# The MLP's first matrix on rows not yet multiplied by the norm's root, with the shift as two more moving columns

## The reference, cut to what matters

```python
x = x + gate1 * (merged @ w_o[l])

u2 = rmsnorm(x, norm_mlp[l]) * (1.0 + scale2) + shift2
h = jnp.square(jax.nn.relu(u2 @ w_ff1[l]))
x = x + gate2 * (h @ w_ff2[l])
```

## Time and profile before

| | us |
|---|---|
| three runs | 982.01, 984.34, 984.48 |
| median | 984.34 |
| span of the profiled execution (first to last instruction) | 980.8 |
| PE busy | 934.8 (95%) |
| POOL busy | 739.2 (75%) |
| DVE busy | 665.4 (68%) |
| ACT busy | 492.7 (50%) |

### The profile page before, as it was taken

One profiled execution on the slowest core, in us unless ns is written; L12 is line 12 of the kernel. 1 busy time (PEld: TensorE's weight loads), 2 busy tenths in 40 slices (PEclk: granted clock), 3 DMA queues, 4 the chain that ended last, 5 costly groups with the idle time before them and its releaser, 6 DMA issues.

```text
span 980.8 us, 21945 instructions
## 1 busy us (share of the span) xinstructions
PE 934.8 (95%) x7758; PEld 909.3 (93%) x7758; DVE 665.4 (68%) x1097; ACT 492.7 (50%) x811; POOL 739.2 (75%) x894
## 2 busy tenths in 40 slices
PE   6999899999789999999999999999989999999996
PEld 6898789999779999999899999999988999999996
DVE  4979996765877774652566678886466666888722
ACT  3455556654346665554454455444454444544441
POOL 1486565677687999998677659999956676799973
PEclk9999999999999999999999999999999999999999
DMA  9985555646453557565354444555515444455521
GB/s 374 401 321 178 212 177 210 236 152 246 164 192 130 204 190 273 179 216 209 129 172 155 150 166 172 174 192 194 211 45 178 167 171 155 146 192 194 178 101 43
DMA packets 28222, 185.20 MB, mean 189 GB/s; under 512 B 3027, under 2 KB 5504, under 8 KB 6272
## 3 DMA queue, kind: packets, MB, share of 16 engines
q1 hardware_dynamic: 25832, 167.93, 47.5%
q10 hardware_dynamic: 2328, 16.40, 4.6%
HBM read 183.26 MB, written 1.07 MB: 188 GB/s over the span
## 4 chain that ended last, share of the span: by engine, by line
PE 74%; DVE 16%; issue 5%; ACT 3%; DMA 1%; DVEq 1%; POOL 0%; SPq 0%; POOLq 0%; ACTq 0%
PE mm L544 21%; PE mm L545 21%; PE mm L546 21%; ACT w_hi L1001 1%; PE mm L578 1%; DVE cy L1967 1%; DVE w_lo L1406 1%; PE mm L562 1%; DVE cy L1972 1%; PE ps_s L871 1%; DVE qr L1991 1%; PE ps_o L888 1%; PE ps_o L962 1%; DVE rt L1990 1%; DVE mix_lo L1936 1%
## 5 line engine op out<-in xcount | busy, mean ns | idle before, releaser
L470 POOL TENSOR_TENSOR w_lo<-raw,w_hi 128x256 fp32r<-128x256 f32 x876 | 729.7, 869 | 215.4 <-ACT w_hi L1001 212.9
L544 PE MATMUL mm<-u_hi,w_hi 128*128 128x256 f32 x1616 | 462.2, 286 | 4.6 <-issue 4.4
L545 PE MATMUL mm<-u_lo,w_hi 128*128 128x256 f32 x1616 | 449.5, 278 | 0.0
L546 PE MATMUL mm<-u_hi,w_lo 128*128 128x256 f32 x1616 | 449.4, 278 | 0.0
L1001 ACT ACTIVATE w_hi<-raw 128x1024 fp32r<-128x1024 f32 x291 | 306.2, 1058 | 144.1 <-PE mm L546 139.6
L544 PEld LDWEIGHTS mm<-u_hi,w_hi 128*128 128x128 f32 x1616 | 304.9, 189 | 12.4 <-issue 11.9
L545 PEld LDWEIGHTS mm<-u_lo,w_hi 128*128 128x128 f32 x1616 | 304.0, 188 | 2.0 <-issue 1.9
L546 PEld LDWEIGHTS mm<-u_hi,w_lo 128*128 128x128 f32 x1616 | 304.4, 188 | 0.0
L1406 DVE TENSOR_TENSOR w_lo<-raw,w_hi 128x1024 fp32r<-128x1024 f32 x72 | 103.4, 1436 | 58.0 <-ACT w_hi L1001 55.4
L544 PE MATMUL mm<-mix_hi,w_hi 128*128 128x256 f32 x256 | 71.7, 280 | 1.5 <-DVE mix_lo L1976 1.5
L545 PE MATMUL mm<-mix_lo,w_hi 128*128 128x256 f32 x256 | 71.4, 279 | 0.0
(11 more groups left out here) (292 smaller groups left out, 1331.1 us busy)
## 6 DMA issues: line engine op xcount, KB each, us to landing
raw<-weights SPq DMA_DIRECT2D x145, 1024.0 KB, 4.8
ada_raw<-ada ACTq DMA_DIRECT2D x14, 1024.0 KB, 5.3
ada_raw<-ada SPq DMA_DIRECT2D x6, 1024.0 KB, 12.4
ada_more<-ada SPq DMA_DIRECT2D x4, 1024.0 KB, 12.7
bias<-tab_scratch SPq DMA_DIRECT2D x1, 1536.0 KB, 9.3
dec<-decay ACTq DMA_DIRECT2D x1, 1536.0 KB, 8.8
x<-xT SPq DMA_DIRECT2D x1, 1024.0 KB, 9.9
out<-x SPq DMA_DIRECT2D x4, 256.0 KB, 2.3
```

Of the source, the lines that this page charges most:

```text
L470: ins = nc.gpsimd.tensor_tensor(w_lo[:, s, at], r[:, at], hi[:, at], ALU.subtract)
L544: nc.tensor.matmul(dst, wh, rhs_hi(k), start=a, stop=False)
L545: nc.tensor.matmul(dst, wh, rhs_lo(k), start=False, stop=False)
L546: i = nc.tensor.matmul(dst, wl, rhs_hi(k), start=False, stop=b)
```

## The change

With a = gain * (1 + scale2), u2 @ w is r * ((a x) @ w) + shift2 @ w. So:

- `u_hi`/`u_lo` now hold a x, without r and without shift. ACT (from x, scale `a_mix`) and DVE (`row_lo`, L1509) write them slice by slice within the w_o product. `make_u` and `make_u_hi` are gone.
- Two more columns stand behind the 256 tokens in each slice of u: shift2 (hi and lo) and zero. Each of the 768 matmuls of the first matrix moves 258 columns; the 257th output column is shift2 @ w.
- PE goes from the w_o product straight into the first two units. The statistic's matmuls stand behind the seventh slice of these, the spread behind the third unit. No `keep_warm` there.
- In `up_turn` DVE copies the 257th column to `wsum`, and multiplies the bank by r (kept in `row1`) into `z_h`, which lies in PSUM; ACT takes relu(z + wsum) from there, squares it, and only then makes the next `w_hi`. DVE makes `h_full` = (z + wsum) * relu, in PSUM too, and `h_lo`.
- The eight sums of gate2's row move into turns 2, 4, 6, 8, 14, 16, 20, 22 of the first matrix, their two loads behind turns 7 and 10 of ACT. DVE's loop over the turns is written out in full, ACT's by half.

```diff
+U_PITCH = T + 32
+U_WIDE = T + 2
...
-    u_hi = keep("u_hi", [P, KC, T], F32R)
-    u_lo = keep("u_lo", [P, KC, T], F32R)
+    u_hi_all = keep("u_hi", [P, KC, U_PITCH], F32R)
+    u_lo_all = keep("u_lo", [P, KC, U_PITCH], F32R)
+    u_hi, u_lo = u_hi_all[:, :, 0:T], u_lo_all[:, :, 0:T]
...
-    h_full = p2("h_full", [P, 2, T])
+    row1 = p2("row1", [P, T])
+    wsum = p2("wsum", [P, 2, 1])
...
+    z_h = ps_s[0].rearrange("p (e t) -> p e t", e=2)
+    h_full = ps_t[:, :].rearrange("p (e t) -> p e t", e=2)
...
+    GATE2_AT = [2, 4, 6, 8, 14, 16, 20, 22]
+    GATE2_LOAD = {7: 22, 10: 23}
...
-                    dst = mm[oo % 4][:, 0:T]
+                    dst = mm[oo % 4][:, 0:w]
...
-        norm_stat(1, O_F1)
-
-        first_units(2, U_F1, O_F1, u_ready(1))
-
+        def stat_behind(k):
+
+            if k == KC - 2:
+                stat(1)
+
+        uhw = lambda k: u_hi_all[:, k, 0:U_WIDE]
+        ulw = lambda k: u_lo_all[:, k, 0:U_WIDE]
+        pe.wait_ge(S["shift_zero"], 2)
+        pe.wait_ge(S["shift_lo"], 1)
+        first_units(2, U_F1, O_F1, u_ready(1), behind=stat_behind, w=U_WIDE)
         for i in range(2, 8):
-            unit(None, U_F1 + i, O_F1 + i, uh, ul)
+            unit(None, U_F1 + i, O_F1 + i, uhw, ulw, w=U_WIDE)
+            if i == 2:
+                spread(1)
         with pe.Fori(0, 3) as g:
             for i in range(8):
-                unit(g, U_F1 + 8 + i, O_F1 + 8 + i, uh, ul)
+                unit(g, U_F1 + 8 + i, O_F1 + 8 + i, uhw, ulw, w=U_WIDE)
...
-            high(None, U_WO + j + SLOTS)
-            if j in (2, 4):
-                ada_load(act, 21 + j // 2)
+            if j == 0:
+                ada_read(act, 5 * KC - 1)
+                A(u_hi_all[:, :, T], mod[:, SHIFT2, :], ACT.Copy).then_inc(S["shift_hi"], 1)
+            if j < KC - 1:
+                high(None, U_WO + j + SLOTS)
             act.wait_ge(taken[o % 4], o // 4 + 1)
+            A(u_hi[:, j, :], x[:, j, :], ACT.Identity, scale=a_mix[:, 1, j:j + 1]).then_inc(S["uhi_ready"], 1)
             square_x(1, j, x[:, j, :])
+        high(None, U_F1 + SLOTS - 1)
         root(1)
-        ada_read(act, 4 * KC - 1)
-        make_u_hi(1, SHIFT2)
 
 
         def up_turn(g, base):
             for i in range(8):
                 c, o, f = U_F1 + base + i, O_F1 + base + i, base + i
-                act.wait_ge(S["unit_done"], lin(g, 8, c + 1))
                 if f >= 2:
                     act.wait_ge(S["hl_ready"], lin(g, 8, f - 1))
-                A(relu_h[:, f % 2, :], mm[o % 4][:, 0:T], ACT.Relu).then_inc(taken[o % 4], 1)
-                high(g, c + SLOTS)
+                act.wait_ge(S["wsum_ready"], lin(g, 8, f + 1))
                 act.wait_ge(taken[o % 4], lin(g, 2, o // 4 + 1))
+                A(relu_h[:, f % 2, :], z_h[:, f % 2, :], ACT.Relu, bias=wsum[:, f % 2, 0:1]).then_inc(S["relu_made"], 1)
+                act.wait_ge(S["relu_made"], lin(g, 8, f + 1))
                 dst = h_hi[:, f, :] if g is None else h_hi[:, bass.ds(g * 8 + f, 1), :][:, 0, :]
                 A(dst, relu_h[:, f % 2, :], ACT.Square).then_inc(S["hh_ready"], 1)
-
-        up_turn(None, 0)
-        with act.Fori(0, 3) as g:
-            up_turn(g, 8)
+                high(g, c + SLOTS)
+                if g is None and f in GATE2_LOAD:
+                    ada_load(act, GATE2_LOAD[f])
...
+        for tile in (u_hi_all, u_lo_all):
+            V.memset(tile[:, :, T + 1].bitcast(F32), 0.0).then_inc(S["shift_zero"], 1)
...
+            if j == 1:
+                dve.wait_ge(S["shift_hi"], 1)
+                V.tensor_tensor(u_lo_all[:, :, T], mod[:, SHIFT2, :], u_hi_all[:, :, T].bitcast(F32), ALU.subtract)\
+                    .then_inc(S["shift_lo"], 1)
+            if j:
+                row_lo(1, j - 1, a_mix[:, 1, j - 1:j])
+            if j == KC - 1:
+                row_lo(1, j, a_mix[:, 1, j:j + 1])
             low(None, U_WO + j + SLOTS)
             if j:
                 add_square(1, j - 1)
-            if j < KC - 1:
-                ada_step(5 * KC + j)
         variance(1)
         dve.wait_ge(S["rstd_ready"], 2)
-        make_u(1, lambda k: a_mix[:, 1, k:k + 1], SHIFT2)
-
-        ada_step(6 * KC - 1)
+        V.tensor_copy(row1[:, :], ps_o[:, 0:T]).then_inc(S["row1_kept"], 1)
+        dve.wait_ge(S["row1_kept"], 1)
 
         def up_turn(g, base):
             for i in range(8):
                 c, o, f = U_F1 + base + i, O_F1 + base + i, base + i
-                dve.wait_ge(taken[o % 4], lin(g, 2, o // 4 + 1))
-                own(V.tensor_tensor(h_full[:, f % 2, :], relu_h[:, f % 2, :], relu_h[:, f % 2, :], ALU.mult))
+                dve.wait_ge(S["unit_done"], lin(g, 8, c + 1))
+                V.tensor_copy(wsum[:, f % 2, 0:1], mm[o % 4][:, T:T + 1]).then_inc(S["wsum_ready"], 1)
+                V.tensor_tensor(z_h[:, f % 2, :], mm[o % 4][:, 0:T], row1[:, :], ALU.mult).then_inc(taken[o % 4], 1)
+                if f:
+                    low(g, c - 1 + SLOTS)
+                if f in GATE2_AT:
+                    ada_step(5 * KC + GATE2_AT.index(f))
+                dve.wait_ge(S["relu_made"], lin(g, 8, f + 1))
+                own(V.scalar_tensor_tensor(h_full[:, f % 2, :], z_h[:, f % 2, :], wsum[:, f % 2, 0:1], relu_h[:, f % 2, :],
+                                           ALU.add, ALU.mult))
                 dve.wait_ge(S["hh_ready"], lin(g, 8, f + 1))
                 sl = (lambda t: t[:, f, :]) if g is None else (lambda t: t[:, bass.ds(g * 8 + f, 1), :][:, 0, :])
                 V.tensor_tensor(sl(h_lo), h_full[:, f % 2, :], sl(h_hi).bitcast(F32), ALU.subtract)\
                     .then_inc(S["hl_ready"], 1)
-                low(g, c + SLOTS)
-
-        up_turn(None, 0)
-        with dve.Fori(0, 3) as g:
-            own.enter(g, 8)
-            up_turn(g, 8)
-            own.leave(3)
+
+        for base in range(0, 32, 8):
+            up_turn(None, base)
+        low(None, U_F2 - 1 + SLOTS)
...
-SPREAD_USED = {0: ("t_ready", KC), 1: ("t_ready", 2 * KC), 2: ("row_kept", 1), 3: ("y_ready", KC),
+SPREAD_USED = {0: ("t_ready", KC), 1: ("row1_kept", 1), 2: ("row_kept", 1), 3: ("y_ready", KC),
...
-    nc = bacc.Bacc("TRN2", target_bir_lowering=False, num_devices=1)
+    nc = bacc.Bacc("TRN2", target_bir_lowering=False, num_devices=1, dynamic_dma_scratch_size=1024)
```

36 lines of the change are left out of this document (9 added, 27 removed).

## The result

| | before | changed |
|---|---|---|
| median (lowest to highest), 20 runs each | 984.41 us (981.22 to 995.34) | 990.86 us (987.30 to 998.40) |
| ratio to before, 95% interval | | 1.006 (1.0039 to 1.0082) |
| profiled execution: time, span | 984.34, 980.8 us | 990.66, 988.8 us |

A forecast was written before the change was run, and what follows sets the result against it. PE, busy 95% of 980.8 us, bounds the kernel, so only gaps can be won. Saving 11.45 - 1.1 - 0.6 - 0.6 - 5.8 = 3.35 us, off the median 984.34: 981.0; range 976.8 to 985.0 for 8 in 10 runs.

The forecast's parts named there:

- The gap and w_o's idle: Before the first matrix: 2.8 us of the w_o product and the 7.25 us gap behind it would go.
- First units, statistic, spread, start waits: First matrix: first two units 1.4 us shorter; statistic costs 1.1, spread 0.6, stalls together 5.8.
- the 0.35 of unit 11: First matrix: unit 11 would start 0.35 us late, part of the 5.8 us of stalls.
- DVE and POOL: First matrix: DVE's z and h_full take 0.42 us, DVE has 7 us to spare; POOL's quarters fall to about 0.77.
- B: Rival: POOL does not speed up in the first matrix from 0.945 us a quarter; saving 2.1, 982.2; chance 0.14.
- C: Rival: DVE bounds the first matrix from 2.35 us a turn; at 2.6, 8 us slower, 992.5; chance 0.12.
- Rival D: New stalls in the first matrix bring another fall of the clock, costing up to 1.8 us: 982.6; chance 0.11.
- E: Rival: unit 0 of the first matrix still waits for the root, so PE is not freed; given no chance.
- A: First matrix: start stall smaller (975.2 with none) or larger (986.8 at twice); with the forecast 977.5 to 983, chance 0.63.
- Two more columns on 768 matmuls: First matrix: two columns cost 0.8 ns a matmul by proportion, 0.6 us in all, between 0 and 2.0.
- What follows does the same work: Stages behind the first matrix do the same work; POOL comes with slack, but no unit waited there: no change.
- the base: Whole kernel: the saving was taken off the median 984.34 of three times, 982.01 to 984.48.

The follow-up runs named there:

- e1: The kernel before with only the smaller dynamic DMA scratch: 986.03 us, ratio 0.9974 to the kernel before.
- e2: The kernel before with the smaller DMA scratch and slices of u 288 elements apart instead of 256, matmuls still 256 wide: 998.29 us, ratio 1.0104.
- e9: The kernel before with the smaller DMA scratch and slices of u 320 elements (1280 bytes) apart instead of 256: 985.81 us, ratio 1.0005.
- e5: The changed kernel with seven of gate2's eight sums and their loads back in the w_o product: 996.75 us, ratio 1.0106 to the kernel before.
- e6: The changed kernel with slices of u 320 elements (1280 bytes) apart instead of 288 (1152): 986.81 us, ratio 1.0016 to the kernel before.
- e13: The changed kernel with one short matmul of 128 columns ahead of the MLP's second matrix: 991.72 us, ratio 1.0032 to the kernel before.
- e14: The changed kernel with two short matmuls of 128 columns ahead of the MLP's second matrix: 995.38 us, one execution.
- e10: The changed kernel with slices 320 apart, w_hi of the first turns made earlier, both shift halves beside u_hi: 980.24 us, ratio 0.9962 to the kernel before.
- e12: e10 with unit 11's w_hi one turn earlier and the third and fourth gate sums at turns 8 and 12: 981.15 us, ratio 0.9978 to the kernel before.
- e3: The changed kernel with 256 columns instead of 258 in the first matrix, shift left out: 991.32 us, ratio 1.0024 to the kernel before.

## Why the prediction was wrong, by its steps

- **The gap and w_o's idle** (forecast -10.05 up to the start of the first matrix): right. Measured -11.0. The w_o product gave 4.9 where 2.8 was forecast (1.1 of it at its head), less 1.2 in the heads' outputs, where the half-clock stretch now lies. In the other profiles with this w_o product and without its sums the same stretch of the program took 51.4 to 53.5 us, against 62.4 to 62.8 in before, e1, e2 and e9, so 0.9 is within the scatter. e5 shows the sums' part of it.
- **First units, statistic, spread, start waits** (forecast 6.7 - 0.6 = +6.1 in the first matrix): right in kind, 1.7 too much. 9.8 less the pace's 768 x (120.3 - 113.2) = 5.4 leaves 4.4. The waits came at the four units named, the first two ended by DVE's w_lo and POOL's as said: 1.66, 1.55, 0.78 and 0.87, forecast 1.6, 1.85, 1.05 and 0.95; the 0.35 of unit 11 did not come. Statistic and spread fit into the stream for less than the 1.7 forecast.
- **DVE and POOL**: z and h_full at 0.42 and 0.49 against 0.42. POOL sped up to 0.838, not below 0.8. Rivals B and C did not come: from unit 8 on PE is not idle, and DVE waits for it. h_full, which adds a column per partition, came nearer to the 0.48 of x<-mm,mod,x, which has one too, than to L1731, which the forecast took. h_lo with an input in PSUM is 0.424, z with one 0.423, the 0.42 that was forecast. The 62 cycles more for an input in PSUM that the Trainium skill gives ("VectorE: DVE Perf Modes", TRN2 errata) do not show: the shortest h_lo of the kernel before, both inputs in SBUF, took 0.424 too. Rival D did not come: the clock is 1.00 from 283 to 381 us. E is refuted by 282.55. A's 977.5 to 983 is not 981.0 with 2 us either way, which would be 979 to 983.
- **The failed step: "Two more columns on 768 matmuls: ... 0.8 ns, 0.6 us in all".** Measured 5.4 us against 0.6, with 2.0 as the upper bound. I priced width by proportion, while the matmuls go by a step: 258 columns are 7 ns slower than the fast pace of 256, whether the slices are 1152 or 1280 bytes apart (e6). And I took the edit for columns only, when it also moved the slices of u from 1024 to 1152 bytes apart, which I did not price at all. On the first matrix that adds nothing to the width's charge; its cost is in the next step.
- **The second step that failed: "What follows does the same work".** The same tile u serves every projection of the program. The new distance took 5.5 us there (e2, e6, e9). The second matrix took 3.4 more, which the runs tie to the moment at which the stream starts (e13, e14) and not to anything that the change added to that stage. That part of the profiled 8.0 is luck of the two executions. So is the base, if the crowds are what I take them for: 984.34 is from three executions of the lower one. 2.1 at the start and -1.6 at the end are scatter.

Added up from the forecast -3.35: +4.8 for the width within the stage, +5.5 for the distance elsewhere, +3.4 for the second matrix, +0.5 for start and end, -0.2 ahead of layer 1, -0.9 and -1.7 for the steps that came out better: +8.05, measured +8.0.

The upper end of the range, 985.0, took in B, D and the near side of C. None of the rivals had PE's own matmuls slower, because all of them asked who keeps PE waiting. In a kernel where PE is 95% busy, 6% on 768 matmuls took back half of the 11 us that the change had won.

Part of the forecast's saving can be had: e10, with slices 320 apart, weights made ahead of the row, and columns beside u_hi alone, ran 0.38% under the kernel before (0.10 to 0.65%). It is the lowest of several variants, and e12, which builds on it, has an interval that reaches 1.

## What to carry to other kernels

Where PE is the bound, price a change first by what it does to one matmul: its width, and the distance between the slices it reads, for every stage that reads the tile. Put a tile's padding where the slices keep a distance that was measured fast (here 1024 or 1280 bytes, not 1152), and test it by changing that number alone. And when a change fills a gap, look for the work that stood behind the gap's end: here the next weights were made only behind the chain that had filled it, and four waits of 0.8 to 1.7 us took its place until they were moved ahead.

## What was not expected of the hardware

- The same 256 column matmuls have two steady paces, 113.3 and 117.8 ns, at full clock and with PE never idle. In the traces no stream went from one to the other without an interruption, and two short matmuls ahead of a stage changed it for 87 us (e14). What in the start decides it stays open.
- With u's slices 1152 bytes apart the fast pace did not occur in any of the eight profiles with that distance; 116.6 ns took its place (e3). With 1024 and 1280 it did.
- 258 columns run at 120.6 ns at 1280 bytes and at 120.3 at 1152, 272 at 123.2.
- A half-clock stretch of 14 to 17 us at the start of layer 1 came in six of sixteen profiles, and those spent 5 to 7 us more on layer 1's matmuls on u than their like (71 matmuls from 731 to 745 us in e2, 108 in the changed kernel at full clock). The mean granted clock was below 0.989 in five of these six and in none of the others; among all executions it was so in 16 of 104 of the kernel before and in 7 of 20 of the changed one. What brings it stays open.
